# One core, two model blocks in one kernel: the router of the second block's experts and both ends of the gate-table stage rearranged

## The reference

```python
def chunk(xc):                                    # first block, 128 tokens at a time
    q = (xc @ w_pq).reshape(P_CHUNK, P_HEADS, 2, P_DK // 2)
    s = jnp.einsum('thpd,hpkd->thpk', q, sub_keys)
    s_top, i_top = lax.top_k(s, P_TOPK)           # 16 of 128 keys, for both halves
    cand = s_top[..., 0, :, None] + s_top[..., 1, None, :]
    best, ci = lax.top_k(cand.reshape(P_CHUNK, P_HEADS, P_TOPK * P_TOPK), P_TOPK)
    e1 = jnp.take_along_axis(i_top[..., 0, :], ci // P_TOPK, axis=-1)
    e2 = jnp.take_along_axis(i_top[..., 1, :], ci % P_TOPK, axis=-1)
    expert = e1 * N_KEYS + e2                     # one of 128 x 128
    gate = jax.nn.softmax(best.astype(jnp.float32), axis=-1)
    act = jax.nn.gelu(jnp.einsum('thkd,td->thk', u_tab[expert], xc), approximate=False)
    return jnp.einsum('thk,thkd->td', gate * act, v_tab[expert])
...
g_logits = t @ w_rg + b_rg                        # second block: 4 groups of 4 experts
g_idx = jnp.argmax(g_logits, axis=-1)
e_logits = (t @ w_re + b_re).reshape(n, N_GROUPS, EXPERTS_PER_GROUP)
in_group = jnp.take_along_axis(e_logits, g_idx[:, None, None], axis=1)[:, 0]
top_v, top_i = lax.top_k(in_group, TOP_K_INNER)   # two experts of the best group
w_sel = jax.nn.softmax(top_v, axis=-1) * w_grp    # w_grp: the group's softmax share
for e in range(N_EXPERTS_2):
    a = jax.nn.silu(t @ w_gate[e]) * (t @ w_up[e])
    y = y + combine[:, e:e + 1] * (a @ w_down[e])
```

## Time and profile before

| | us |
|---|---|
| median of three runs | 1877.17 |
| profiled execution, its own time | 1874.72 |
| span of its instructions | 1872.9 |
| PE busy | 1798.3 (96%) |
| DVE busy | 1026.5 (55%) |
| ACT busy | 619.1 (33%) |
| POOL busy | 159.4 (9%) |

### The profile page before, as it was taken

One profiled execution on the slowest core, in us unless ns is written; L12 is line 12 of the kernel. 1 busy time (PEld: TensorE's weight loads), 2 busy tenths in 40 slices (PEclk: granted clock), 3 DMA queues, 4 the chain that ended last, 5 costly groups with the idle time before them and its releaser, 6 DMA issues. The chain is left out here.

```text
span 1872.9 us, 23879 instructions
## 1 busy us (share of the span) xinstructions
PE 1798.3 (96%) x9068; PEld 1402.1 (75%) x9068; DVE 1026.5 (55%) x2064; ACT 619.1 (33%) x888; POOL 159.4 (9%) x81
## 2 busy tenths in 40 slices
PE   7999989999998999799999999999898999999997
PEld 4887546778887999677788888888776888555554
DVE  2569745220899876777677667776324432411113
ACT  2111254111101666233454454554255120122222
POOL 1200000000000998100000000000000000000000
PEclk9999999999999999899999999999999999899999
DMA  9366221233443222455555555554532335399992
GB/s 369 142 265 262 76 90 46 95 130 120 173 159 110 72 89 99 146 182 199 179 180 187 193 181 192 187 182 156 209 130 104 121 129 233 143 428 426 428 427 100
DMA packets 33335, 343.61 MB, mean 183 GB/s; under 512 B 3952, under 2 KB 4464, under 8 KB 5104
## 3 DMA queue, kind: packets, MB, share of 16 engines
q1 hardware_dynamic: 32256, 340.16, 48.1%
q10 hardware_dynamic: 1008, 2.45, 0.3%
HBM read 340.49 MB, written 2.10 MB: 183 GB/s over the span
## 5 line engine op out<-in xcount | busy, mean ns | idle before, releaser
L559 PE MATMUL psD<-xh,ring 128*128 128x256 f32 x1856 | 410.3, 382 | 8.3 <-DVE arena L2070 4.9
L559 PEld LDWEIGHTS psD<-xh,ring 128*128 128x128 f32 x1856 | 352.0, 191 | 65.2 <-issue 14.8
L844 PE MATMUL psY<-ring_r,work_r 128*128 128x512 f32 x1536 | 370.5, 397 | 11.2 <-DVE ring_r L1855 11.2
L844 PEld LDWEIGHTS psY<-ring_r,work_r 128*128 128x128 f32 x1536 | 283.3, 190 | 80.4 <-issue 17.9
L1146 ACT ACTIVATE arena<-psD 128x512 f32<-128x512 f32 (+4 forms) x187 | 132.4, 715 | 599.2 <-PE psD L559 456.5
L1146 ACT ACTIVATE ring_r<-ring 128x1024 fp32r<-128x1024 f32 x196 | 200.2, 1055 | 171.4 <-PE psY L844 113.0
L830 PE MATMUL psD<-xh_r,ring_r 128*128 128x512 f32 x544 | 194.1, 397 | 0.0
L559 PE MATMUL psD<-arena,ring 128*128 128x256 f32 x704 | 166.2, 396 | 7.7 <-DMA ring<-in_w_in 4.4
L1855 DVE TENSOR_TENSOR ring_r<-ring,ring_r 128x1024 fp32r<-128x1024 f32 x128 | 160.7, 1255 | 15.1 <-ACT ring_r L1146 15.0
L559 PEld LDWEIGHTS psD<-arena,ring 128*128 128x128 f32 x704 | 132.8, 191 | 38.8 <-issue 8.5
L832 PE MATMUL psD<-xh_r,ring_r 128*128 128x256 f32 x544 | 152.9, 281 | 0.0
(11 more groups left out here) (271 smaller groups left out, 1983.5 us busy)
## 6 DMA issues: line engine op xcount, KB each, us to landing
ring<-in_tables SPq DMA_DIRECT2D x68, 1024.0 KB, 4.8
arena<-in_experts SPq DMA_DIRECT2D x30, 2048.0 KB, 16.2
ring<-in_w_in SPq DMA_DIRECT2D x20, 2048.0 KB, 8.6
ring<-in_experts SPq DMA_DIRECT2D x18, 2048.0 KB, 14.1
ring<-in_early_v SPq DMA_DIRECT2D x30, 1024.0 KB, 4.8
ring<-in_w_mod SPq DMA_DIRECT2D x12, 2048.0 KB, 8.1
ring<-in_early_u SPq DMA_DIRECT2D x9, 2048.0 KB, 7.8
ring<-in_mid_u SPq DMA_DIRECT2D x12, 1024.0 KB, 4.9
```

Source lines behind the costliest of these rows:

```text
L559: last = nc.tensor.matmul(dst, a, b, start=(i == 0), stop=(i == len(pairs) - 1))
L844: last = nc.tensor.matmul(psY[:, t * D + h * 512:t * D + (h + 1) * 512], wgt[:, b, t * P:(t + 1) * P], v[:, h * 512:(h + 1) * 512], start= ...
```

## The change

**Table stage, its start.** The second exponential moves from the last GELU of the 36 early columns to two GELUs earlier; DVE starts its search when the first half of the scores is out, and no longer zeroes psY (the first expert's first matmuls overwrite it, `start=first`). PE takes 17 middle steps ahead of the first table (`mid_done`, with `LEAD`) and 5.6 a table after that, in place of 6 ahead of each. **Its end.** ACT rounds the first two `v` columns as soon as the two last tables have given up the buffers; DVE subtracts the first and, after the last table, does its own product with the early columns ahead of ACT's copy; the second zeroing is gone. `mid_gate` comes in two halves and eight quarters, POOL's split in 16 pieces, one an expert from the twelfth on. **Router.** PE takes the logits feature-major (8 products of 20 by 256) and turns them after ACT has copied them; ACT loads its table for the exponential ahead of time with a one-element instruction; DVE's chain doesn't wait for the exponential, and after the places comes at once the first seat and its one-hot; weights, rounds and the other seats follow. `keep` is 3 and 2 matmuls instead of 7 and 6, and PE reads the number of rounds after the first four turns. Two semaphores that ACT raised in one go (`qp_ready`, `ih`) are replaced by waits on the tiles themselves.

```diff
+LEAD = 12
...
+def mid_done(n):
+    return LEAD + (MID * K - LEAD) * n // (T // 8) if n else 0
...
-    add("router", 1, "dve")
+    add("router", 1, "act")
...
-                    sp.wait_ge(mid_gated, 1)
+                    sp.wait_ge(mid_gated, 2)
...
-            pe.wait_ge(y_zero, 1)
             for n in range(T // 8):
-                for i in range(MID * K * n // (T // 8), MID * K * (n + 1) // (T // 8)):
+                for i in range(mid_done(n), mid_done(n + 1)):
                     mid_step(i)
...
-                                                    start=False, stop=False, skip_group_check=True)
+                                                    start=first and i == 0, stop=False, skip_group_check=True)
...
-            pe.wait_ge(y_zero, 2)
-            with pe.Fori(0, PRE // 4) as it:
+            pe.wait_ge(mid_ready, MID // 2)
+            for e in range(8):
+                early_v(e, e, e == 0)
+            with pe.Fori(1, PRE // 4) as it:
                 for e in range(8):
...
-            pe.wait_ge(h_split, 1)
+            pe.wait_ge(h_split, K)
...
-            for t in range(TT):
-                last = group(ps[:, 20 * t:20 * (t + 1)], [(hT[:, k, t * P:(t + 1) * P], w_router[:, k, :])
-                                                          for k in range(K)],
-                             after=None if t else (h_part, 2 * K))
-            last.then_inc(tile_ready, 1)
+            group(ps[0:20, 0:T], [(w_router[:, k, :], hT[:, k, :]) for k in range(K)],
+                  after=(h_part, 2 * K)).then_inc(tile_ready, 1)
...
+                if n == 0:
+                    pe.wait_ge(tile_free["act"], readers[:TILE["router"] + 1].count("act"))
+                    for t in range(TT):
+                        last = nc.tensor.transpose(aux(0)[:, 20 * t:20 * (t + 1)], logitsT[0:20, t * P:(t + 1) * P],
+                                                   ident[0:20, 0:20])
+                    last.then_inc(logits_ready, 1)
+            keep(3, aux(3))
             pe.wait_ge(mask_ready, 1)
...
+                pe.wait_ge(col_ready, it * 4 + (t + 1))
...
-            keep(6, psD[1])
-            pe.wait_ge(rounds_ready, 1)
-            fours = pe.value_load(rounds[0:1, 1:2], min_val=PAIRS // 4, max_val=PAIRS // 4 * ROUNDS)
+            keep(2, psD[1])
...
-                    pe.wait_ge(y_zero, 3)
+                    pe.wait_ge(y_zero, 1)
                 turn(0, t, t > 0)
+            pe.wait_ge(rounds_ready, 1)
+            fours = pe.value_load(rounds[0:1, 1:2], min_val=PAIRS // 4, max_val=PAIRS // 4 * ROUNDS)
...
+                if g == 3:
+                    act.wait_ge(tile_free["act"], readers[:TILE["scores"] + n + 1].count("act"))
+                    act.sem_inc(sc_ready, 1)
...
-                if n in (TOPU // 3, TOPU // 2 - 1):
-                    t = n // (TOPU // 2 - 1)
+                if n in (TOPU // 3, TOPU // 2 - 3):
...
+                if n + 1 < T // 8:
+                    gates_out(it, h)
...
+                else:
+                    act.wait_ge(col_loaded[0], 16 + MID_LOADS[0])
+                    act.wait_ge(gb_done, n + 3)
+                    fn(v_hi[h], early_half(col_slot, h), ACT.Copy).then_inc(v_hi_ready, 1)
+            gates_out(T // 16 - 1, 1, early_gated)
...
-            act.wait_ge(h_part, 3 * K)
+            fn(warm, ones[:, 0:1], ACT.Exp)
+            ps = take(TILE["router"])
+            fn(logitsT[0:20, :], ps[0:20, 0:T], ACT.Copy).then_inc(tile_free["act"], 1)
...
-            pool.wait_ge(mid_gated, 2)
             pool.wait_ge(mid_used, MID // 2)
-            nc.gpsimd.tensor_copy(h_hi, hT).then_inc(h_hi_ready, 1)
-            pool.wait_ge(h_hi_ready, 1)
-            nc.gpsimd.tensor_tensor(h_lo, hT, h_hi.bitcast(F32), ALU.subtract).then_inc(h_split, 1)
+            pool.wait_ge(mid_gated, 6)
+            for k in range(K):
+                pool.wait_ge(v_done, 12 + 2 * k)
+                nc.gpsimd.tensor_copy(h_hi[:, k, :], hT[:, k, :]).then_inc(h_hi_ready, 1)
+                pool.wait_ge(v_done, 13 + 2 * k)
+                pool.wait_ge(h_hi_ready, k + 1)
+                nc.gpsimd.tensor_tensor(h_lo[:, k, :], hT[:, k, :], h_hi[:, k, :].bitcast(F32),
+                                        ALU.subtract).then_inc(h_split, 1)
...
-            dve.wait_ge(sc_ready, 1)
...
+                dve.wait_ge(sc_ready, t + 1)
...
-            dve.wait_ge(stat_used, STATS.index("x1") + 1)
-            nc.vector.memset(psY[:, :], 0.0).then_inc(y_zero, 1)
...
-            dve.wait_ge(mid_ready, MID // 2)
-            nc.vector.memset(psY[:, 1024:2048], 0.0).then_inc(y_zero, 1)
-            gate_early(T // 16 - 1, 1)
...
+            def early_rest(nth, e):
+                v_rest(nth, e % 2, early_half(col_lo, e), early_half(col_slot, e))
...
+            def mid_gate(i, lo, n):
+                a = gate_all[:, TOPU + 8 * i + lo:TOPU + 8 * i + lo + n, :]
+                tt(a, a, mid_act[i][:, lo:lo + n, :], ALU.mult).then_inc(mid_gated, 1)
+            early_rest(0, 0)
+            gate_early(T // 16 - 1, 1, gb_done)
             dve.wait_ge(early_gated, T // 8 + 2)
-            def mid_gate(i):
-                a = gate_all[:, TOPU + 8 * i:TOPU + 8 * (i + 1), :]
-                tt(a, a, mid_act[i], ALU.mult).then_inc(mid_gated, 1)
-            for e in range(8):
-                early(e, e, False)
-                if e in (1, 3, 5):
...
+            for e in range(2, 16):
+                early(e, e % 8)
+                if e == 2:
+                    mid_gate(2, 4, 4)
+                if 4 <= e < 12:
+                    mid_gate((e - 4) // 4, 2 * (e % 4), 2)
+            dve.wait_ge(mid_gated, 10)
+            with dve.Fori(2, PRE // 4) as it:
...
-            ps = take(TILE["router"])
+            dve.wait_ge(logits_ready, 1)
             lg = rt[:, 16:56].rearrange("p (t n) -> p t n", t=TT)
-            tt(lg, ps[:, 0:40].rearrange("p (t n) -> p t n", t=TT),
-               b_router.rearrange("p (a n) -> p a n", a=1).broadcast_to([P, TT, 20]), ALU.add).then_inc(tile_free["dve"], 1)
-            dve.wait_ge(tile_free["dve"], readers[:TILE["router"] + 1].count("dve"))
+            seq(tt(lg, aux(0)[:, 0:40].rearrange("p (t n) -> p t n", t=TT),
+                   b_router.rearrange("p (a n) -> p a n", a=1).broadcast_to([P, TT, 20]), ALU.add))
             places4 = iota[:, 0:4].rearrange("p (a n) -> p a n", a=1).broadcast_to([P, TT, 4])
...
-            dve.wait_ge(rexp, 1)
-            seq(nc.vector.tensor_reduce(r2(74), r24(0), AX.X, ALU.add))
-            seq(nc.vector.reciprocal(r2(74), r2(74)))
...
+            dve.wait_ge(place_ready, 1)
+            ps = aux(2)
+            seq(stt(mask, mask, -FAR, ps[:, 0:2 * NEXP].rearrange("p (t e) -> p t e", t=TT), ALU.mult, ALU.add))
+            seq(ts(seat[:, :, 0:NEXP], mask, FAR, None, ALU.add))
+            tt(hots, iota64, seat0, ALU.is_equal).then_inc(hot_ready, 1)
...
+            nc.vector.tensor_copy(seat_col, comb[:, :, 0:2]).then_inc(col_ready, 1)
...
+            seq(nc.vector.tensor_reduce(r2(150, 1), ps[:, 2 * NEXP:3 * NEXP], AX.X, ALU.max))
...
+                if r:
+                    mark(ts(seat[:, :, r * NEXP:(r + 1) * NEXP], mask, FAR - SEAT * r, None, ALU.add))
+                mark(nc.vector.tensor_copy(seat_w[:, :, r * NEXP:(r + 1) * NEXP], comb))
...
```

107 lines of the change are left out of this document (50 added, 57 removed).

## The result

The kernel after takes 1848.25 us (median of four runs, 1847.36 to 1849.97), the kernel before 1877.39 beside it: ratio 0.9843, 95% interval 0.9826 to 0.986, 29.1 us less where 21.6 were forecast. The profiled execution has a span of 1845.4 us against 1872.9.

A forecast was written before the change was run, and what follows sets the result against it. The prediction took PE, busy 96% of the span, as the bound. Its terms summed to -21.6 us from the profiled 1874.72, giving 1853.1, and with the runs' median 2.45 higher 1855.6 us; range 1848 to 1862.

The forecast's parts named there:

- The clock: Charge for falls to half clock in three remaining gaps, at the tables' start and end and the router: +3.6 us.
- Seams of the tables and of POOL's split: Terms for the tables' start and end, POOL's split and the middle gates: -5.6, -2.6, -2.6, -9.4, +1.5, +0.3 us.
- POOL gave nothing back: In the tables, part of PE's early lead was expected to be lost to POOL's pace: 0.6 us.
- Half of a fall in each gap: At each of three remaining PE gaps, half of the 2.4 us that a clock fall cost was charged.
- POOL's stall: POOL's split in 16 pieces removes PE's 6.86 us stall and 2.5 us of half clock: -9.4 us; pieces cost +1.5.
- Router and what follows: From the logits on, ACT's first copy of gathered tokens comes 7.1 us earlier; PE's register load costs +0.3.
- The 0.3 for PE's register load: Between turns four and five, PE's moved register load may let its queue run dry: +0.3 us, bounds 0 to 1.93.
- the clock never falls: Rival: no clock fall in the three remaining gaps, 3.6 us less, 1852.0 us; chance 0.22.
- the shared port: Rival: POOL and DVE share more than allowed, tables at 4.33 and pieces costing 4.3 us, 1860.9 us; chance 0.14.
- no transfer held a turn: Rival, in the turns after the router: transfers hold the turns and swallow the router's gain, 1861.2 us; chance 0.08.
- the tables kept step: Rival: tables fall out of step, POOL's product and DVE's comparison locked at 5.38 us a table, 1890.6 us; chance 0.04.
- The row from 1603 to 1604: At the router's narrow logits, a window with PE busy 1.00 yet clock 0.76, read as busy being no safeguard.

The follow-up runs named there:

- gap2: The kernel after with two more DVE instructions of 1.2 us ahead of the first v column's weights, lengthening PE's idle at the tables' end; 1852.38 us.
- gap1: The kernel after with one more DVE instruction of 1.2 us ahead of the first v column's weights; 1847.94 us.
- split_whole: The kernel after with POOL's rounding and subtraction of hT as two whole instructions started at column 12; 1856.21 us.
- seams_only: The kernel after with the router of the kernel before; 1859.95 us.
- router_again: Repeat of the kernel before with the router of the kernel after and without the ih wait in the second block; 1864.69 us.
- before_again: The kernel before, unchanged, profiled a second time; 1879.87 us.
- after_third: The kernel after, unchanged, run a third time; 1849.9 us.
- fill_all: The kernel after with filling matmuls rearranged in the router and added in three idle stretches, DVE's psY zeroing and ACT's register load moved later; 1841.44 us.
- fill_all_again: Repeat of fill_all, unchanged, beside the kernel after on one chip; 1840.35 us.

## Why the prediction missed

The mechanisms of its sum were there; the step that failed is "The clock", at both places: at the tables it charged for falls that did not come, and at the router it charged 1.2 us and put the old router's own falls at nothing. Measured is the mean over profiled executions.

- Seams of the tables and of POOL's split: the sum said -18.4, plus 2.4 for two gaps. Measured 693.45 - 711.38 = -17.9, means over eight and four executions. The start (4.67 with the 0.5 of chance ahead of it), the period of 4.223, the 3.63 us and the pieces' 1.5 (1.5 taken) came out as worked; POOL gave nothing back (0.6 taken), and the 2.4 were not paid: 0 at the end of the tables, two falls in twelve at the start, 0.3 on average. "Half of a fall in each gap" left out the length of the gap. At the end of the tables the clock fell in five of five executions with 4.20 or 4.37 us of idle and in none of fourteen with 1.68 or 2.94, and gap2 and gap1 (one execution each) differ from the kernel after in nothing else.
- POOL's stall: -9.4 and +1.8 foretold, -7.6; split_whole measures 6.6 from the other side.
- Router and what follows: -7.1 + 0.3 + 1.2 = -5.6 foretold, -9.9 measured. The path itself was right: `hrow_lo` 5.34 us nearer to the logits (5.1), ACT's copy 7.37 nearer (7.1), not by the load but because `keep` at half clock took as long. The 0.3 for PE's register load did not show. What I did not price is that the old router falls to the low clock by chance too, and more often than in the one execution I read: 277.3 us from the logits to the end on average, against 273.6 in that one, of which 1.3 were low clock in the first turn (244.80 - 243.46). The new one's draws cost 2.5 on average (267.4 over 264.9), more than the 1.2 charged.

So of the 7.5 us by which the gain was larger than forecast 1.9 are the seams' charge and 4.3 the router; the other 1.3 are not placed. Of the rivals, "the clock never falls" was right for the seams and wrong for the router; the shared port cost no more than taken; no transfer held a turn (28.31 us a turn with and without the change); the tables kept step (4.223).

The Trainium skill, TensorE: Matmul & The Clock Gate, section What's actually happening, ties the clock to how busy PE has recently been. The filled gaps agree: with PE busy in them the clock is 1.00 where it is 0.50 without. The row from 1603 to 1604, which I had read as speaking against it, is no single case: in all three executions with the old logits (20 columns a product) the clock fell 2.1 to 4.2 us behind their start, with PE busy, and in none of sixteen with the wide ones within 11 us. By the busy records alone those three do not agree with the page. Up to there nothing else differs: of the 20 us ahead of the logits PE is busy for 19.21 in both. Windows over the logits of seams_only, then of router_again:

```profile
1584.00:1588.00 4.00, 4.00 (x20) 3.92 (x20) 0.55 (x2) 0.00 (x0) 0.00 (x0) 0.51 0.84 360
```

```profile
1596.00:1600.00 4.00, 4.00 (x21) 1.87 (x20) 2.43 (x7) 1.02 (x3) 0.00 (x0) 1.00 1.03 442
```

`hrow_lo` comes 15.74, 16.75 and 17.15 us behind the logits with the narrow products (before, before_again, seams_only), the later the sooner the clock fell, and 10.38 to 10.40 with the wide ones. So the prediction's remark that the wide logits should help was right, and its sum had put it at nothing. The width was not changed by itself, so why busy records go with a falling clock stays open.

## What to carry to other kernels

Profile a kernel several times before pricing its stalls, list where the clock is low in each, and compare stretches between two marks, not spans: here one trace of the kernel before was 5 us faster than the next. A gap of PE that is cut down (4.37 to 1.68 us here) gives back its length and also the half clock behind it. One that can't be cut is worth filling with products that wait for nothing, and such filling should go only when the gap goes.

## What the hardware showed that was not expected

- Two executions of one kernel differed by 11.1 us in time at the low clock and by 6.1 us in span. The falls come at the same few places (near 200 and 250 us, the second block's two gaps, the router, the last stage), and in none of nineteen executions between 260 and 590 us, where PE never waits longer than 1.5 us.
- Two wide `keep` products (3.40 us at half clock instead of 1.7) ended in a risen clock in one execution (0.84 at 1596); the same two left it low until 1605.3 in another (after_third), so filling behind a gap is a chance. In the filled gaps of the second block the clock stayed up in both executions (fill_all, fill_all_again).
- POOL's subtraction of 256 columns (0.74 us) stretches a DVE cast from 0.29 to 0.83 us, and POOL's rounding (0.40) to 0.47; both times the cast ends 0.15 us behind POOL.
